# Small tables by TensorE transposes, and four modulation chunks as TensorE products, in a two-layer trunk kernel

## The chip, the cores and the metric

The kernel runs on one core of a Trainium2 chip. The metric is the time of one execution on the device in microseconds (us). The engines are named as the profile names them: PE (TensorE, with PEld its weight loads), DVE (VectorE), ACT (ScalarE), POOL (GpSimd) and SP (SyncE, which here only issues DMAs). ACTq and SPq are the instruction queues of ACT and SP with the DMAs that they issue. All data are float32.

## What is computed

The reference is a trunk of two layers on 256 tokens of 1024 channels. Each layer is modulated by six vectors of 1024 values, computed from one conditioning vector `c`:

```python
cond = jax.nn.silu(c)
for i in range(DEPTH):                                # 2
    mod = (cond @ mod_w[i] + mod_b[i]).reshape(B, 6, D_MODEL)   # mod_w[i] is 1024 x 6144
    h = modulate(rmsnorm(x, g[0]), mod[:, 0], mod[:, 1])        # shift, scale
    y = diff_attention(h, ...) if i == 0 else mlstm_layer(h, ...)
    x = x + mod[:, 2][:, None, :] * rmsnorm(y, g[1])
    h = modulate(rmsnorm(x, g[2]), mod[:, 3], mod[:, 4])
    y = swiglu(h, ...) if i == 0 else moe_swiglu(h, ...)        # 8 experts, top 2
    x = x + mod[:, 5][:, None, :] * rmsnorm(y, g[3])
```

The attention needs a scalar `lam_full`, made of exponentials of two sums over `attn_lambda`. The mLSTM layer multiplies its channels by three tables of 4x4 blocks (`mlstm_w_q`, `_k`, `_v`, 512 blocks each), and all three results by `mlstm_w_gate` (6144 x 8). The router of the experts is `moe_w_router` (1024 x 8).

## The kernel before

Five engine programs are written out by hand and meet at semaphores. All large weights come through one ring in SBUF of 7 slots of 2 MB (`ring`, `SLOTS`). `PLAN` lists the chunks in order, 512 columns of all 1024 rows each for the input matrices. It begins with four chunks of layer 0's `mod_w` (channels 0 to 2047, the first shift and scale), and then come the six chunks of the attention's input matrix, `attn_in` 0 to 5, with two more modulation chunks behind each of `attn_in` 0, 1 and 2 and one behind each of 3 and 4. Counted from 0, index 3 of `PLAN` is the fourth modulation chunk, 4 is `attn_in` 0, 7 is `attn_in` 1, 10 is `attn_in` 2, 13 is `attn_in` 3, 15 is `attn_in` 4 and 17 is `attn_in` 5. SP issues them strictly in that order (L418), and from the eighth on waits first until the chunk seven before has been read (L416).

The start runs as follows.

- SP (L403 to L413) loads the small vectors as rows of 128 (`rows`), eight DMAs, then `x`. PE turns `rows` (L794), DVE copies the result to `vecs` (L1242), and ACT makes `cond` of it with Silu (L550).
- ACT (L552 to L557) then issues seven DMAs: three tables of blocks (`qkv_blocks`, L553, runs of 4 floats), the gate weights (`w_gates`, L554, runs of 8 floats), the gate bias (L555), the router weights (`w_router`, L556, runs of 8 floats) and the router bias (L557). Only behind these stands in its program the exponential of the lambda step (L560), and behind that the squares of `x` and the scaling of `x` (L526, L530).
- DVE, after `vecs`, starts the lambda step (L1246, L1247), prepares some constants, waits for ACT's exponential and ends the lambda step (L1255 to L1257). Then come the variances (L1195) and the four modulation chunks (`mod_chunk`): eight instructions of 128x512 for each, a multiply (L1169) and seven multiply-adds (L1171) into `mod_acc`.
- PE sums each chunk's accumulator over the partitions with four 128x32 by 128x128 matmuls (`mod_sum`, L730), each in another group of 32 columns of the array, so that chunk j lands in row j of four row groups of PSUM bank 7. Then it turns the rows (`mod_turn`, L737), and the sixteen 128x128 tiles of the scaled `x` (`transposes`, L747). DVE adds the bias (L1185), makes `mul_c` (L1267) and writes the modulated, turned input `hT` (`modulated`, L1205).
- From there on PE multiplies the six `attn_in` chunks (L786 for 0 to 3, L815 for 4 and 5), 32 large matmuls each. A float32 matmul stands in the trace as two records, a transpose as one. Between the `attn_in` chunks PE sums the modulation chunks that DVE has accumulated meanwhile; the softmax stage follows.

The later stages (feed-forward, mLSTM, eight experts) are not touched, apart from what the semaphores count.

Of the kernel before, what the change touches and what calls it, by code (L numbers as in the profile page):

```python
# [19 lines left out]
ALU = mybir.AluOpType  # L20
# [6 lines left out]
P = 128  # L27
# [21 lines left out]
MOD_PARTS = {0: (0, 4, 12), 1: (0, 12)}  # L49

# [73 lines left out]
def trunk(nc, a, out):  # L124
    with ExitStack() as ctx:
# [26 lines left out]
        cond = sb("cond", [P, KT])  # L152
# [72 lines left out]

        hid = area(FT * S, after_acc).rearrange("p (k s) -> p k s", k=FT)
# [55 lines left out]
        cond_ready = sem("cond_ready")  # L282
        acc_ready = sem("acc_ready")
# [82 lines left out]
        for m, f, n, r in PLAN:  # L366
            j = f // WC
            if r == "dve":
                n_mod += 1
                read_by.append((acc_ready, n_mod))  # L370
# [30 lines left out]
        def sp_program(sp):  # L401

            sp.wait_ge(rows_clear, 1)  # L403
            cw = a["mlstm_conv_w"][0]
            sp.dma_start(rows[0:64, 0, :], cw.rearrange("j (t p) -> (j t) p", p=P)).then_inc(rows_loaded, 16)
# [3 lines left out]
            sp.dma_start(rows[0:8, 1, :], a["c"][0].rearrange("(t p) -> t p", p=P)).then_inc(rows_loaded, 16)  # L409
            sp.dma_start(rows[8:72, 1, :], a["norm_g"].rearrange("l i (t p) -> (l i t) p", p=P)).then_inc(rows_loaded, 16)  # L410
            sp.dma_start(rows[72:73, 1, :], a["attn_subln"]).then_inc(rows_loaded, 16)
            sp.dma_start(rows[0:96, 2, :], a["mod_b"].rearrange("l (t p) -> (l t) p", p=P)).then_inc(rows_loaded, 16)
# [21 lines left out]
        def pool_program(pool):  # L434
# [7 lines left out]
            pool.memset(rows, 0.0).then_inc(rows_clear, 1)  # L442
            pool.memset(exponent, -0.5)
# [52 lines left out]
            pool.wait_ge(small_loaded, 16 * 7)  # L496
# [15 lines left out]
        def act_program(act):  # L512
# [39 lines left out]
            for m, name in enumerate(("mlstm_w_q", "mlstm_w_k", "mlstm_w_v")):  # L552
                act.dma_start(qkv_blocks[:, m], a[name][0].rearrange("(t g) i o -> (g i) t o", g=P // 4)).then_inc(small_loaded, 16)  # L553
            act.dma_start(w_gates[:], a["mlstm_w_gate"][0].rearrange("(k p) n -> p k n", p=P)).then_inc(small_loaded, 16)  # L554
            act.dma_start(b_gates[:], a["mlstm_b_gate"].broadcast_to([P, 2 * MH])).then_inc(small_loaded, 16)  # L555
            act.dma_start(w_router[:], a["moe_w_router"][0].rearrange("(k p) n -> p k n", p=P)).then_inc(small_loaded, 16)  # L556
            act.dma_start(b_router[:], a["moe_b_router"].broadcast_to([P, E])).then_inc(small_loaded, 16)  # L557

            act.wait_ge(lam_ready, 1)
            act.activation(lam_e, lam_s, ACT.Exp).then_inc(lam_ready, 1)  # L560
            for t in range(TT):
                squares_x(0, t)
            for t in range(TT):
                normed_x(t, t + 1)

# [142 lines left out]
        def pe_program(pe):  # L708
# [15 lines left out]
            def mod_sum(layer, j, n):  # L724

                pe.wait_ge(acc_ready, n + 1)
# [5 lines left out]
                ins.then_inc(mod_summed, 1)  # L732

# [89 lines left out]
            pe.wait_ge(t_free, 2)  # L823

# [83 lines left out]
            def gate_products(t):  # L908
                pe.wait_ge(u_free, FILLS["qkv"] + 2 * (t + 1))
                if t == 0:  # L910
                    pe.wait_ge(small_loaded, 16 * 7)
                    pe.wait_ge(t_free, 5)
# [230 lines left out]
        def dve_program(dve):  # L1143
# [17 lines left out]
            def mod_chunk(layer, j, n):  # L1161
# [7 lines left out]
                link(dve.tensor_scalar(acc, w[:, 0], cond[:, 0:1], None, ALU.mult))  # L1169
                for k in range(1, KT):  # L1170
                    ins = dve.scalar_tensor_tensor(out=acc, in0=w[:, k], scalar=cond[:, k:k + 1], in1=acc,  # L1171
                                                   op0=ALU.mult, op1=ALU.add)
                    if k < KT - 1:
                        link(ins)
# [94 lines left out]
            modulated(0)  # L1269
            for j in range(6):  # L1270
# [408 lines left out]
```

## Time and profile before

| | before |
|---|---|
| median of 3 runs | 2170.09 us (2169.73 to 2179.38) |
| span of the profiled execution | 2170.9 us |
| PE busy | 1724.5 us, 79% |
| DVE busy | 474.3 us, 22% |
| ACT busy | 185.4 us, 9% |
| HBM read | 480.86 MB, 222 GB/s over the span |
| first matmul of `attn_in` starts | 89.44 us |
| first matmul of `attn_in` 3 starts | 132.42 us |

The result files give a time for each run, and the trace holds one more execution, whose span is given beside them. The page has each engine's busy share in 40 slices of 54.3 us, the chain of work that ended last, and the costliest groups of instructions. A group's "idle before" is the time its engine stood still ahead of it, with what ended the wait. The first slice is the one that the change touches, and it is read best instruction by instruction.

### The profile page before, as it was taken

The numbers are of one execution on the slowest core, as the hardware profiler recorded it, in microseconds if no ns is written. First come the engines' busy times: TensorE is split into PE (matmuls) and PEld (weight loads), VectorE is DVE, ScalarE is ACT, GpSimd is POOL, SyncE is SP. The second block draws the span as 40 slices with busy tenths as digits, with TensorE's granted clock in tenths as the row PEclk, the third lists the DMA queues.
The fourth block names the chain that finished last, engine by engine and source line by source line (L and its number), as shares of the span: only waits on it lengthen the run. The fifth ranks groups of instructions, "written<-read, shape, count | busy, mean of one in ns | idle before, by whom it ended". The sixth has DMA issues, their size and how long they took to land.

```text
span 2170.9 us, 18533 instructions
## 1 busy us (share of the span) xinstructions
PE 1724.5 (79%) x7558; PEld 1060.3 (49%) x7559; DVE 474.3 (22%) x1045; ACT 185.4 (9%) x404; POOL 33.2 (2%) x70
## 2 busy tenths in 40 slices
PE   0496799998978886687999968699996848768486
PEld 0374388844746633326996323299632313232232
DVE  0677235401563413101000000100001000100101
ACT  0104100001102101100000001000001001010010
POOL 0000000000020000000000000000000000000000
PEclk9997899999999887898999989999997979979798
DMA  9593239673401043397645429966651997969886
GB/s 300 179 379 140 78 144 342 218 283 117 155 1 39 0 160 111 140 402 278 220 166 198 152 82 336 396 238 227 237 195 55 396 368 268 402 243 399 324 309 252
DMA packets 219137, 484.72 MB, mean 223 GB/s; under 512 B 17545, under 2 KB 20002, under 8 KB 218914
## 3 DMA queue, kind: packets, MB, share of 16 engines
q1 hardware_dynamic: 205090, 481.46, 59.9%
q8 instruction: 118, 1.93, 0.4%
q10 hardware_dynamic: 13824, 0.47, 0.4%
q14 instruction: 105, 0.86, 0.1%
HBM read 480.86 MB, written 1.05 MB: 222 GB/s over the span
## 4 chain that ended last, share of the span: by engine, by line
PE 70%; issue 10%; DMA 8%; DVE 7%; ACTq 2%; ACT 1%; SPq 1%; POOL 0%; DVEq 0%; POOLq 0%
PE ps L786 15%; PE ps L1084 13%; PE ps L1054 13%; PE ps L1103 9%; DMA ring<-in_moe_w_down 7%; PE ps L773 6%; PE ps L1028 2%; PE ps L1131 2%; PE ps L815 1%; DMA ring<-in_moe_w_up 1%; DVE arena L1171 1%; ACTq L553 1%; PE ps L1063 1%; DVE hT L1205 1%; SPq L399 1%
## 5 line engine op out<-in xcount | busy, mean ns | idle before, releaser
L1054 PE MATMUL ps<-ring,arena 128*64 128x512 f32 x672 | 318.0, 631 | 47.9 <-issue 47.5
L1103 PE MATMUL ps<-ring,arena 128*64 128x512 f32 (+3 forms) x1120 | 322.6, 597 | 30.7 <-DMA ring<-in_moe_w_down 30.7
L786 PE MATMUL ps<-hT,ring 128*128 128x256 f32 x1472 | 327.3, 384 | 9.3 <-DVE hT L1205 7.6
L1055 PE MATMUL ps<-ring,arena 128*64 128x512 f32 x672 | 318.4, 631 | 0.0
L786 PEld LDWEIGHTS ps<-hT,ring 128*128 128x128 f32 x1472 | 281.4, 192 | 51.9 <-DVE hT L1205 8.8
L1084 PE MATMUL ps<-arena,ring 128*128 128x208 f32 (+1 forms) x1792 | 291.5, 326 | 0.0
L1084 PEld LDWEIGHTS ps<-arena,ring 128*128 128x128 f32 x1792 | 291.2, 190 | 0.0
L1103 PEld LDWEIGHTS ps<-ring,arena 128*64 128x64 f32 (+3 forms) x1120 | 110.2, 147 | 233.1 <-issue 179.5
L1054 PEld LDWEIGHTS ps<-ring,arena 128*64 128x64 f32 x672 | 94.1, 144 | 236.1 <-issue 234.3
L1028 PE MATMUL ps<-arena 128*128 128x128 f32 (+2 forms) x256 | 51.3, 384 | 151.1 <-issue 151.1
L773 PE MATMUL ps<-ring,arena 128*128 128x512 f32 x368 | 161.4, 601 | 1.5 <-DVE arena L1338 1.5
L1171 DVE SCALAR_TENSOR_TENSOR arena<-ring,cond,arena 128x512 f32<-128x512 f32 x168 | 126.3, 752 | 6.0
L1028 PEld LDWEIGHTS ps<-arena 128*128 128x128 f32 x256 | 49.5, 279 | 159.3 <-issue 159.2
L773 PEld LDWEIGHTS ps<-ring,arena 128*128 128x128 f32 x368 | 71.2, 194 | 92.2 <-issue 90.3
L1593 DVE TENSOR_TENSOR arena<-arena,ps 64x512 f32<-64x512 f32 x42 | 29.0, 690 | 360.7 <-ACT arena L645 360.7
L1055 PEld LDWEIGHTS ps<-ring,arena 128*64 128x64 f32 x672 | 94.1, 144 | 0.0
L1598 DVE TENSOR_TENSOR arena<-arena,ps 128x208 f32<-128x208 f32 (+1 forms) x56 | 19.9, 355 | 271.9 <-ACT arena L655 271.9
L730 PE MATMUL ps<-arena,ones_col 128*32 128x128 f32 x192 | 10.5, 306 | 72.3 <-DVE arena L1171 72.3
L1614 DVE TENSOR_TENSOR arena<-arena,ps 128x512 f32<-128x512 f32 x32 | 19.8, 682 | 215.0 <-PE ps L1131 215.0
L1587 DVE TENSOR_SCALAR arena<-ps,mul_c,modc 128x64 f32<-128x64 f32 (+2 forms) x64 | 21.2, 373 | 162.2 <-PE ps L1028 162.2
L1131 PE MATMUL ps<-arena 64*128 64x512 f32 (+3 forms) x80 | 44.3, 694 | 9.7 <-DVE arena L1606 5.3
L645 ACT ACTIVATE arena<-ps 64x512 f32<-64x512 f32 x42 | 24.8, 590 | 300.8 <-PE ps L1055 300.7
(262 smaller groups left out, 872.5 us busy)
## 6 DMA issues: line engine op xcount, KB each, us to landing
ring<-in_moe_w_gate SPq DMA_DIRECT2D x56, 2048.0 KB, 20.3
ring<-in_moe_w_up SPq DMA_DIRECT2D x56, 2048.0 KB, 18.8
ring<-in_moe_w_down SPq DMA_DIRECT2D x56, 2048.0 KB, 21.3
ring<-in_mod_w SPq DMA_DIRECT2D x24, 2048.0 KB, 11.9
ring<-in_mlstm_w_in SPq DMA_DIRECT2D x8, 2048.0 KB, 8.5
ring<-in_attn_w_in SPq DMA_DIRECT2D x6, 2048.0 KB, 10.5
ring<-in_ffn_w_gate SPq DMA_DIRECT2D x5, 2048.0 KB, 12.9
ring<-in_ffn_w_up SPq DMA_DIRECT2D x5, 2048.0 KB, 12.3
```

The lines of the kernel that those rows point to most:

```text
L399: sp.dma_start(slot_down(s), src).then_inc(landed[s], 16)
L645: act.activation(hx[0:width, j % 2, 0:WC], ps[0:width, 2 * (j % 2)], ACT.Silu).then_inc(silu_moe, STEP)
L773: ins = pe.matmul(ps[:, 4 + 2 * t + c], lhs[:, first + k, t * P:(t + 1) * P], w[:, k, c * 512:(c + 1) * 512], start=(first + k == 0), stop ...
L786: ins = pe.matmul(dst, w[:, k, c * P:(c + 1) * P], hT[:, k, :], start=(k == 0), stop=(k == KT - 1))
L1028: ins = pe.matmul(ps[:, i, j * S:j * S + wide], xn[:, t, k * P:(k + 1) * P], sel[:, t, 0:wide], start=(t == 0), stop=(t == TT - 1))
L1054: pe.matmul(ps[0:width, b], x_k, wg[:, k, :], start=(k == 0), stop=(k == KT - 1))
L1055: ins = pe.matmul(ps[low, b + 1], x_k, wu[:, k, :], start=(k == 0), stop=(k == KT - 1))
L1084: ins = pe.matmul(dst, w[:, k, c * P:(c + 1) * P], xg[:, k, 0:width], start=(k == 0), stop=(k == KT - 1))
L1103: ins = pe.matmul(ps[r, 4 + 2 * st + n], eh[:, ft, st * P:st * P + sw[st]], w[:, k, n * 512:(n + 1) * 512], start=(ft == 0), stop=(ft == E ...
L1131: ins = pe.matmul(ps[:, 4 + 2 * t + n], scat[0:sw[st], st, t * P:(t + 1) * P], ye[0:sw[st], st, n * 512:(n + 1) * 512], start=(st == 0), s ...
L1171: ins = dve.scalar_tensor_tensor(out=acc, in0=w[:, k], scalar=cond[:, k:k + 1], in1=acc, op0=ALU.mult, op1=ALU.add)
L1593: dve.tensor_tensor(hx[0:width, j % 2, 0:WC], hx[0:width, j % 2, 0:WC], ps[second_half(width), 2 * (j % 2) + 1], ALU.mult).then_inc(hx_rea ...
```

## The change

1. The seven small loads on ACT go to the head of its program, ahead of `cond`. Five of them change form: the blocks, the gate weights and the router weights are loaded as contiguous rows of 2 or 4 KB into scratch areas (16 rows for each of the three block tables, 48 for the gate weights, 8 for the router weights). PE turns them with 20 transposes (`turn_tables`: 4 + 8 + 8) into PSUM banks 4 and 5, reading every fourth or every eighth element of a row. ACT copies the result to the old tables in three instructions. A new semaphore holds back PE's softmax stage until these copies are done.
2. ACT's squares and scaling of `x` come ahead of the table copies and of the lambda exponential. DVE's end of the lambda step moves behind `modulated(0)`.
3. The first four modulation chunks are no longer accumulated by DVE. PE multiplies them directly (`mod_product`): for each of 8 row tiles and each of 4 column quarters a matmul of a 128x32 window of `cond` by 128x128 of the chunk. `cond` is for that widened to 63 columns per row tile with the values in column 31 and zeros around, set by two more POOL instructions. The transposes of `x` come between the first product and the second, the turned tables between the second and the third.
4. The eight loads of `rows` are issued in another order. The kernel is built with a smaller scratch area for DMAs issued by POOL, of which it has none.

```diff
+            for m, name in enumerate(("mlstm_w_q", "mlstm_w_k", "mlstm_w_v")):
+                act.dma_start(block_rows[IT * m:IT * (m + 1)],
+                              a[name][0].rearrange("(t g) i o -> t (g i o)", g=P // 4)).then_inc(tables_loaded, 16)
+            act.dma_start(table_rows[0:3 * IT], a["mlstm_w_gate"][0].rearrange("(k p) n -> k (p n)", p=P)).then_inc(tables_loaded, 16)
+            act.dma_start(router_rows[0:KT], a["moe_w_router"][0].rearrange("(k p) n -> k (p n)", p=P)).then_inc(tables_loaded, 16)
...
+            act.wait_ge(consts, 1)
             act.wait_ge(u_free, 1)
-            act.activation(cond[:], c_cols, ACT.Silu).then_inc(cond_ready, 1)
...
-            act.dma_start(w_gates[:], a["mlstm_w_gate"][0].rearrange("(k p) n -> p k n", p=P)).then_inc(small_loaded, 16)
...
+            act.activation(cond[:, :, 31], c_cols, ACT.Silu).then_inc(cond_ready, 1)
+            for t in range(TT):
+                squares_x(0, t)
+            for t in range(TT):
+                normed_x(t, t + 1)
+
+            act.wait_ge(tables_turned, 3)
...
             act.wait_ge(lam_ready, 1)
             act.activation(lam_e, lam_s, ACT.Exp).then_inc(lam_ready, 1)
-            for t in range(TT):
-                squares_x(0, t)
-            for t in range(TT):
-                normed_x(t, t + 1)
...
+            def mod_product(layer, j, n):
+
+                i = chunk(f"mod{layer}", j * WC)
+                w = slot_up(i % SLOTS)
+                for k in range(KT):
+                    for q in range(4):
+                        ins = pe.matmul(ps[32 * q:32 * (q + 1), 7, 0:P], cond[:, k, 31 - j:63 - j], w[:, k, q * P:(q + 1) * P],
+                                        start=(k == 0 and j in MOD_PARTS[layer]),
+                                        stop=(k == KT - 1 and j + 1 in MOD_PARTS[layer]))
+                ins.then_inc(mod_summed, 1)
+
+            def turn_tables():
+
+                pe.wait_ge(tables_loaded, 16 * 5)
+                for o in range(4):
+                    ins = pe.transpose(ps[:, 4, o * 3 * IT:(o + 1) * 3 * IT],
+                                       block_rows[0:3 * IT].rearrange("r (c o) -> r o c", o=4)[:, o], ident[0:3 * IT, 0:3 * IT])
+                ins.then_inc(tables_turned, 1)
...
-            mods = 0
-            for j in range(4):
-                mod_sum(0, j, mods)
-                mods += 1
+            pe.wait_ge(cond_ready, 1)
+            mod_product(0, 0, 0)
+            transposes_x(0)
+            mod_product(0, 1, 1)
+            turn_tables()
+            for j in range(2, EARLY):
+                mod_product(0, j, j)
+            mods = EARLY
             mod_turn(1)
-            transposes_x(0)
...
-            dve.wait_ge(lam_ready, 2)
-            link(dve.tensor_tensor(neg_lam, lam_e[:, 1:2], lam_e[:, 0:1], ALU.subtract))
-            link(dve.tensor_scalar(neg_lam, neg_lam, -LAMBDA_INIT, None, ALU.add))
             for t in range(TT):
                 variance(t)
             dve.wait_ge(cond_ready, 1)
-            mods = 0
-            for j in range(4):
-                mod_chunk(0, j, mods)
-                mods += 1
-
+            mods = EARLY
             modulation(1, 0, 4)
```

## Rows read from the trace of the kernel before

**Rows 1.** The page: its first line and the granted clock in 40 slices.

```profile
span 2170.9 us, 18533 instructions
PEclk9997899999999887898999989999997979979798
```

**Rows 2.** The chain that ended last, 0 to 150 us: start, us, what.

```profile
8.64 6.95 ACTq L553
15.62 11.47 ACTq L553
27.12 11.84 ACTq L554
38.99 14.27 ACTq L555
...
89.44 27.89 PE ps L786 x128
```

**Rows 3.** The timeline, 0 to 90 us: start, us, engine, line, what, idle before.

```profile
8.20 0.21 ACT L550 ACTIVATE cond<-vecs 128x8 f32<-128x8 f32 x1 [5.69 <-DVE vecs L1242]
...
54.40 1.28 ACT L560 ACT_TABLE_LOAD   x1 [45.99 <-issue]
...
56.00 0.16 DVE L1256 TENSOR_TENSOR small<-small 128x1 f32<-128x1 f32 x1 [46.06 <-ACT small L560]
...
57.88 2.29 ACT L530 ACTIVATE arena<-x,small 128x1024 f32<-128x1024 f32 x2
...
58.09 0.49 DVE L1169 TENSOR_SCALAR arena<-ring,cond 128x512 f32<-128x512 f32 x1
...
81.88 0.66 PE L730 MATMUL ps<-arena,ones_col 128*32 128x128 f32 x8 [5.26 <-DVE arena L1171]
82.60 0.29 DVE L1181 COPY arena<-ps 128x128 f32<-128x128 f32 x1 [0.78 <-PE ps L730]
...
83.22 3.62 PE L747 MATMUL ps<-ident,arena 128*128 128x128 f32 x16
...
83.67 0.17 DVE L1267 SCALAR_TENSOR_TENSOR mul_c<-modc,vecs 128x8 f32<-128x8 f32 x1
85.67 3.71 DVE L1205 TENSOR_SCALAR hT<-ps,mul_c,modc 128x256 f32<-128x256 f32 x8 [1.83 <-PE ps L747]
```

**Rows 4.** SP's chunk loads in index order, each with its issue and time to landing.

```profile
L418 SPq DMA_DIRECT2D ring<-in_mod_w x1: 460/460/460, 5.7 to 5.7; - x1
DMA to landing us min/median/max: 10.3/10.3/10.3
...
L418 SPq DMA_DIRECT2D ring<-in_mod_w x2: 5597/5754/5912, 6.9 to 12.5; - x2
DMA to landing us min/median/max: 21.2/21.4/21.6
...
L418 SPq DMA_DIRECT2D ring<-in_mod_w x2: 5894/5940/5987, 24.2 to 30.2; - x2
DMA to landing us min/median/max: 22.0/22.2/22.4
```

**Rows 5.** Stretches: us, busy of PE, PEld, DVE, ACT, POOL; clock, DMA share, GB/s.

```profile
10.00:50.00 40.00, 0.00 (x0) 0.00 (x0) 0.00 (x0) 0.00 (x0) 0.00 (x0) 1.00 1.10 355
120.00:145.00 25.00, 25.00 (x130) 21.63 (x129) 22.60 (x33) 0.00 (x0) 0.00 (x0) 1.00 1.05 389
150.00:155.00 5.00, 5.00 (x13) 2.26 (x12) 3.70 (x5) 0.00 (x0) 0.00 (x0) 1.00 1.02 408
163.00:217.00 54.00, 35.88 (x168) 23.02 (x167) 38.22 (x117) 24.09 (x102) 0.00 (x0) 0.78 0.38 139
```

**Rows 6.** The timeline, 103 to 176 us: the attention's input matrix and its end.

```profile
117.83 14.08 PE L786 MATMUL ps<-hT,ring 128*128 128x256 f32 x64
...
132.42 14.08 PE L786 MATMUL ps<-hT,ring 128*128 128x256 f32 x64
...
146.43 0.64 PE L730 MATMUL ps<-arena,ones_col 128*32 128x128 f32 x16
...
175.22 0.43 PE L730 MATMUL ps<-arena,ones_col 128*32 128x128 f32 x8
```

**Rows 7.** Groups of instructions, 0 to 180 us: the accumulations on DVE.

```profile
L1171 DVE SCALAR_TENSOR_TENSOR arena<-ring,cond,arena 128x512 f32<-128x512 f32 x84 | 63.2, 752 | 3.0
```

**Rows 8.** The router's matmuls, L1000: weight loads and their durations in ns.

```profile
L1000 PEld LDWEIGHTS ps<-w_router,hT x32: 288/333/338, 844.4 to 850.9; 128*128 128x128 f32 x32
```

More of the change, by code:

```diff
@@ L49 @@
 MOD_PARTS = {0: (0, 4, 12), 1: (0, 12)}
+EARLY = 4
 SLOTS = 7
@@ L151, in trunk @@
         gate_c = sb("gate_c", [P, 4, KT])
-        cond = sb("cond", [P, KT])
+        cond = sb("cond", [P, KT, 63])
         qkv_blocks = sb("qkv_blocks", [P, 3, IT, 4])
@@ L224, in trunk @@
         lam_in = area(4 * DA).rearrange("p (i n) -> p i n", i=4)
+        table_rows = o_nat[:, 0, :]
+        block_rows = o_nat[:, 1, 0:512]
+        router_rows = oT.rearrange("p k s -> p (k s)")[:, 0:D]
         hid = area(FT * S, after_acc).rearrange("p (k s) -> p k s", k=FT)
@@ L282, in trunk @@
         cond_ready = sem("cond_ready")
+        tables_loaded = sem("tables_loaded")
+        tables_turned = sem("tables_turned")
+        tables_ready = sem("tables_ready")
         acc_ready = sem("acc_ready")
@@ L404, in sp_program @@
             cw = a["mlstm_conv_w"][0]
+            sp.dma_start(rows[0:8, 1, :], a["c"][0].rearrange("(t p) -> t p", p=P)).then_inc(rows_loaded, 16)
+            sp.dma_start(rows[8:72, 1, :], a["norm_g"].rearrange("l i (t p) -> (l i t) p", p=P)).then_inc(rows_loaded, 16)
+            sp.dma_start(rows[72:73, 1, :], a["attn_subln"]).then_inc(rows_loaded, 16)
+            sp.dma_start(rows[0:96, 2, :], a["mod_b"].rearrange("l (t p) -> (l t) p", p=P)).then_inc(rows_loaded, 16)
             sp.dma_start(rows[0:64, 0, :], cw.rearrange("j (t p) -> (j t) p", p=P)).then_inc(rows_loaded, 16)
@@ L442, in pool_program @@
             pool.memset(rows, 0.0).then_inc(rows_clear, 1)
+            pool.memset(cond[:, :, 0:31], 0.0)
+            pool.memset(cond[:, :, 32:63], 0.0)
             pool.memset(exponent, -0.5)
@@ L564, in act_program @@
                 normed_x(t, t + 1)
+            act.wait_ge(tables_turned, 3)
+            act.activation(qkv_blocks.rearrange("p m t o -> p (m t) o"),
+                           ps[:, 4, 0:4 * 3 * IT].rearrange("p (o k) -> p k o", o=4), ACT.Copy)
+            act.activation(w_gates[:], ps[:, 5, 0:8 * 3 * IT].rearrange("p (n k) -> p k n", n=2 * MH), ACT.Copy)
+            act.activation(w_router[:], ps[:, 5, 384:384 + E * KT].rearrange("p (n k) -> p k n", n=E), ACT.Copy).then_inc(tables_ready, 1)
+            act.wait_ge(lam_ready, 1)
+            act.activation(lam_e, lam_s, ACT.Exp).then_inc(lam_ready, 1)
             def exps(h):
@@ L732, in mod_sum @@
                 ins.then_inc(mod_summed, 1)
+            def mod_product(layer, j, n):
[13 more added lines that the diff above has]
+                ins.then_inc(tables_turned, 1)
+                for n in range(2 * MH):
+                    ins = pe.transpose(ps[:, 5, n * 3 * IT:(n + 1) * 3 * IT],
+                                       table_rows[0:3 * IT].rearrange("r (c n) -> r n c", n=2 * MH)[:, n], ident[0:3 * IT, 0:3 * IT])
+                ins.then_inc(tables_turned, 1)
+                for e in range(E):
+                    ins = pe.transpose(ps[:, 5, 384 + e * KT:384 + (e + 1) * KT],
+                                       router_rows[0:KT].rearrange("r (c e) -> r e c", e=E)[:, e], ident[0:KT, 0:KT])
+                ins.then_inc(tables_turned, 1)
             def mod_turn(n):
@@ L823, in pe_program @@
             pe.wait_ge(t_free, 2)
+            pe.wait_ge(tables_ready, 1)
             def scores(h):
@@ L1168, in mod_chunk @@
                 acc = mod_acc[:, n % 2]
-                link(dve.tensor_scalar(acc, w[:, 0], cond[:, 0:1], None, ALU.mult))
+                link(dve.tensor_scalar(acc, w[:, 0], cond[:, 0, 31:32], None, ALU.mult))
                 for k in range(1, KT):
-                    ins = dve.scalar_tensor_tensor(out=acc, in0=w[:, k], scalar=cond[:, k:k + 1], in1=acc,
+                    ins = dve.scalar_tensor_tensor(out=acc, in0=w[:, k], scalar=cond[:, k, 31:32], in1=acc,
                                                    op0=ALU.mult, op1=ALU.add)
@@ L1269, in dve_program @@
             modulated(0)
+            dve.wait_ge(lam_ready, 2)
+            link(dve.tensor_tensor(neg_lam, lam_e[:, 1:2], lam_e[:, 0:1], ALU.subtract))
+            link(dve.tensor_scalar(neg_lam, neg_lam, -LAMBDA_INIT, None, ALU.add))
             for j in range(6):
```

23 lines of the change are left out of this document (7 added, 16 removed).

## The prediction

> **What bounds the kernel now.** I read the page first. Its span is 2170.9 us, and the median of the runs shown is 2170.09 us, so the profiled execution stands for them within 0.04%; I make the sum against its span and take 0.8 us off at the end. The change touches only what lies ahead of the softmax stage, so the second view is the chain that ended last, read for the first 150 us. There the reader sees 44.6 us, from 8.64 to 53.28 us, in four issues of DMAs on ACT's queue (6.95 + 11.47 + 11.84 + 14.27 and small gaps) [rows 2]. No engine computes in that time. The third view is the timeline of the same stretch. ACT had made `cond` at 8.4 us, but the next instruction in its program that computes stands behind the seven issues and begins at 54.40. DVE waits 46.06 us for the lambda exponential, and so its four modulation chunks, whose first begins at 58.09, come late too [rows 3]. Each takes some 5.9 us: 0.49 for the first instruction and seven of 752 ns with their gaps [rows 3, 7]. The first `attn_in` matmul starts at 89.44 us [rows 2]. The idle wait and the four accumulations thus stand one behind the other, and both are on the path.
>
> The fourth view is the loads. Chunk 0 is issued at 5.7 and lands 10.3 us later, at 16.0. Index 2 lands at 28.1 (6.9 + 21.2), index 3 at 34.1 (12.5 + 21.6), index 5 at 46.2 and index 6 at 52.6 (30.2 + 22.4) [rows 4]. Once both waits of above are gone, this is what is late next.
>
> **The small loads (part 1).** They are the 16-byte and 32-byte pieces that block ACT's queue. As whole rows there are 16 + 16 + 16 + 48 + 8 of them, each 2 or 4 KB, and the two bias loads keep their form. I take the issue cost per DMA as small as that of SP's first chunk, 0.46 us [rows 4], which makes 3.2 us for seven from about 1.2 us on, over before DVE's `vecs` at 8.2 us, on which `cond` waits [rows 3]. So what they cost beside the rows' loads is nothing; if that cover is gone, see the third rival. They take 44.6 us off ACT.
>
> **The lambda step and the squares (part 2).** The squares and the scaling of `x` then run right behind `cond`, some 4 us for the four instructions and POOL's powers between them (the scaling alone took 2.29 us [rows 3]). `xn` is ready near 16 us, as chunk 0 lands. On DVE the end of the lambda step is two short instructions (one took 0.16 us [rows 3]); in its new place DVE waits for the first `attn_in` result anyway, so I cost it at nothing, and at 0.4 us without that cover. The exponential comes behind the table copies on ACT, near 30 us, and is asked for near 40.
>
> **The products (part 3).** They remove 4 x 5.9 = 23.6 us of DVE work and four `mod_sum`. They add 32 matmuls of 128x32 by 128x128 a chunk. The nearest row is `mod_sum` itself, four such matmuls side by side: 0.66 us after an idle wait, 0.43 us in the midst of work, and 0.64 us for eight of them in the midst of work [rows 3, 6]. The second four thus add 0.21 us. A product of eight fours costs between 0.43 + 7 x 0.21 = 1.9 us and 8 x 0.66 = 5.3 us. I take 2.5 us, near the lower end, since PE will be working with short pauses from 16 us on. The granted clock in this stage is 1.00 in every stretch that I read [rows 5], so the 0.66 against 0.43 does not show in that column. The Trainium skill, "TensorE: Matmul & The Clock Gate", section on the HAM clock gate, says that after idling the array runs at 1.2 GHz until it has been busy; the durations agree with that, the column does not show it. By that rule all products of a PE that keeps pausing would be near the upper end, which is the second rival.
>
> **The turned tables.** The 20 transposes have no row of their own, for they read every fourth or eighth element. The sixteen of `x` took 3.62 us, 0.226 each [rows 3]; the dearest weight load of 128 columns in a short matmul took 0.338 [rows 8]. So 4.5 to 6.8 us, and 4.5 is taken. They stand between the second and the third product. PE's sum to the end of the third product is 16.0 + 3 x 2.5 + 3.6 + 4.5 = 31.6 us. The fourth chunk lands no earlier than that (below), so PE's own work is hidden behind the loads, by little. ACT's three copies delay nobody: PE asks for them only in the softmax stage. `cond`'s two more memsets on POOL, and the new order of the rows' loads, are hidden by the rows' landing and cost nothing.
>
> **The loads, new pace.** While the small pieces were in the queues the core moved 355 GB/s; without them, with the same kind of chunks, 389 GB/s, and 408 for others [rows 5]. A chunk of 2.097 MB thus takes 5.39 us, between 5.14 and the 6.1 of the landings in the present start, (52.6 - 16.0) / 6 [rows 4]. I take 5.39, from the row with the same matrices. Index i then lands at 16.0 + 5.39 i: index 3 at 32.2, index 4 at 37.6, 7 at 53.7, 10 at 69.9, 13 at 86.1, 15 at 96.9.
>
> **The new start.** The fourth product ends at 32.2 + 2.5 = 34.7. From the end of the last `mod_sum` (82.54) to the end of `mul_c` (83.84) are 1.3 us; then `hT` takes 3.71, and no transposes stand between them any more [rows 3]. With the gaps that is 5.1 us, so the first `attn_in` matmul starts at 39.8 instead of 89.44: 49.6 us earlier.
>
> **What is given back.** In the present kernel the four chunks stood in the ring long before, and PE went through `attn_in` at its own pace: the first two took 27.89 us, `attn_in` 3 started at 132.42, and the stage ended at 175.7 [rows 2, 6]. Now PE asks for three chunks' worth of loads each 14.6 us, and they take 16.2. By PE's pace `attn_in` 1, 2 and 3 start at 53.8, 68.2 and 82.8; by the loads no earlier than 53.7, 69.9 and 86.1. DVE frees index 6's slot at about 54.5 + 2 x 5.9 = 66.3, ahead of the time at which SP's queue would carry index 13, so this wait costs nothing. `attn_in` 3 starts at 86.1, 3.3 us of the gain are gone, and from there the loads run ahead again (`attn_in` 4 is asked for at 100.7 and lands at 96.9). The gain is 132.42 - 86.1 = 46.3 us. It then stays: in the softmax stage the loads need 0.38 of their time [rows 5], so the ring fills up in either kernel, and what follows is the same.
>
> **Sum.** 2170.9 - 46.3 = 2124.6 us of span, 2124 us as a median. Bounds: at 5.14 us a chunk PE's pace decides and 49.6 are gained, at best 2120; if also the product costs 1.9, 2119.
>
> **Rivals.**
> - *The loads stay at the pace of the present start*, 6.1 us a chunk, because it was never the small pieces that slowed them. Index 13 lands at 16.0 + 79.3 = 95.3, the gain is 37.1, the time 2133 us. For it: the 355 GB/s stood for 40 us [rows 5]. Against it: 389 and 408 in the same kernel. The Trainium skill, "DMA: Bandwidth & Descriptors", section "Specifications", gives some 358 GB/s as the limit of HBM per core; this trace disagrees with 389 and 408 GB/s. Chance 0.15.
> - *PE is slow in the start.* Products of 5.3 us and transposes of the tables of 6.8: 16.0 + 4 x 5.3 + 3.6 + 6.8 + 5.1 = 52.7. From there PE's pace decides, `attn_in` 3 starts at 95.7, gain 36.7, 2133 us. For it: the row after an idle wait. Against it: the pauses are short. Chance 0.1.
> - *The loads on ACT block it as before.* `cond` now stands behind them; if they took 44.6 us from 1.2 us on, `cond` would come at about 46, and 46 + 10 + 3.6 + 4.5 + 5.1 = 69.2 as the start, a gain of 20, 2150 us. Against it: 104 whole rows in place of thousands of pieces. Chance 0.04.
> - *Slower than before: the fours don't run side by side and each matmul pays a full weight load.* Place: the 128 matmuls of the products, ahead of all. Price: two records of up to 0.338 us each [rows 8], 0.676 a matmul, 86.5 us in all, a start at 16.0 + 86.5 + 3.6 + 4.5 + 5.1 = 115.7 and 2196 us. It decides from 0.47 us a matmul on ((89.44 - 29.2) / 128). Against it: four in 0.43 to 0.66 us [rows 3, 6]. Chance 0.02.
> - The granted clock of the later stages differs from slice to slice of the page, 7 to 9 tenths [rows 1], 0.78 in the softmax stage [rows 5]; it moves the runs shown by up to 9 us. This widens the range and is no case of its own.
>
> **Chances.** Forecast 0.69, the rivals 0.15, 0.1, 0.04, 0.02. A measurement of this kernel can tell about 0.5% (10.9 us) from no change. The forecast and the first three rivals are faster by more than that, less a little for cases between the third and the fourth: faster 0.95, within 0.5% 0.03, slower 0.02. The range takes in both bounds of the load's pace, the second rival and some of the runs' spread: 2116 to 2137 us.
>
> **What would show it.** The first `attn_in` matmul near 40 us and `attn_in` 3 near 86; products of 2 to 3 us each; the wait ahead of the fourth product ended by a DMA; PE waiting one to two us for a chunk ahead of `attn_in` 2 and of 3; 385 GB/s or more from 10 to 100 us; an unchanged time from the softmax stage to the end. It is wrong if ACT still spends over 10 us on issues, if PE waits for `tables_loaded`, if products take over 5 us, or if the later stages differ by more than 5 us.

## The result

| | before | changed |
|---|---|---|
| median | 2171.86 us (2169.73 to 2179.38, 4 runs) | 2124.24 us (2123.46 to 2129.76, 4 runs) |
| ratio to before | | 0.9777, 95% interval 0.9754 to 0.9800 |
| span of the profiled execution | 2170.9 us | 2122.3 us |
| `attn_in` starts | 89.44 us | 42.24 us |
| `attn_in` 3 starts | 132.42 us | 87.81 us |
| `attn_in` 4 starts | 147.00 us | 102.40 us |

The kernel is 47.6 us faster by the medians and 48.6 us by the spans. The four long issues of DMAs on ACT's queue [rows 2] are gone, and all seven now take 3.4 us, from 1.21 to 4.57 us. The timeline of the changed kernel, 0 to 60 us (columns as in [rows 3]), shows what stands in their place:

```profile
3.11 0.58 ACTq L563 DMA_DIRECT2D arena<-in_moe_w_router  x1
...
10.71 0.21 ACT L569 ACTIVATE cond<-vecs 128x8 f32<-128x8 f32 x1
...
15.87 3.64 PE L758 MATMUL ps<-ring,cond 128*32 128x128 f32 x64 [7.13 <-DMA ring<-in_mod_w]
19.44 2.32 PE L792 MATMUL ps<-ident,arena 128*128 128x128 f32 x16
21.69 1.95 PE L758 MATMUL ps<-ring,cond 128*32 128x128 f32 x64
23.57 0.68 PE L767 MATMUL ps<-ident,arena 48*128 48x48 f32 x4
24.09 1.04 PE L771 MATMUL ps<-ident,arena 48*128 48x48 f32 x8
25.06 1.04 PE L775 MATMUL ps<-ident,arena 8*128 8x8 f32 x8
...
28.15 3.64 PE L758 MATMUL ps<-ring,cond 128*32 128x128 f32 x64 [2.05 <-DMA ring<-in_mod_w]
33.57 3.64 PE L758 MATMUL ps<-ring,cond 128*32 128x128 f32 x64 [1.78 <-DMA ring<-in_mod_w]
37.35 0.29 DVE L1230 COPY arena<-ps 128x128 f32<-128x128 f32 x1 [24.17 <-PE ps L758]
...
38.48 3.71 DVE L1254 TENSOR_SCALAR hT<-ps,mul_c,modc 128x256 f32<-128x256 f32 x8
```

L758 are the products, L792 the transposes of `x`, L767 to L775 the turned tables. The reader is to see that the third and the fourth product waited for a DMA; the loads are now what the start waits for. The same kind of product takes 1.95 us once and 3.64 us three times. The stretches (columns as in [rows 5]) show the granted clock beside that, and that the loads run at full pace throughout:

```profile
15.84:19.50 3.66, 3.63 (x65) 3.28 (x65) 0.00 (x0) 0.00 (x0) 0.00 (x0) 1.00 1.06 388
...
21.69:23.60 1.91, 1.91 (x66) 1.71 (x65) 0.00 (x0) 0.00 (x0) 0.00 (x0) 1.00 1.05 387
...
28.15:31.80 3.65, 3.64 (x64) 2.98 (x64) 0.00 (x0) 0.33 (x2) 0.00 (x0) 0.50 1.05 387
33.57:37.20 3.63, 3.63 (x64) 2.96 (x64) 0.00 (x0) 0.00 (x0) 0.00 (x0) 0.50 1.04 385
42.24:47.00 4.76, 4.76 (x11) 3.86 (x12) 0.17 (x2) 0.00 (x0) 0.00 (x0) 0.50 1.05 387
```

At 0.50 the array runs at 1.2 GHz, at 1.00 at 2.4. The first product, behind 7.13 us of waiting, took 3.64 us too, but the column reads 1.00 beside it: there the column and the duration don't agree. The first `attn_in` matmuls, behind a wait of 4.22 us, ran at 0.50 as well: the first two chunks took 30.48 us in place of 27.89 [rows 2].

### The profile page after: what moved, and what is told of

It is laid out like the page before. It is cut to its first block, busy times and chain, and to the rows that moved or that the text cites. A ratio compares the mean times of both kernels' runs of the same rounds, so it can differ in the third digit from the quotient of the medians.

```text
span 2122.3 us, 18995 instructions
## 1 busy us (share of the span) xinstructions
PE 1728.3 (81%) x7802; PEld 1072.5 (51%) x7803; DVE 451.6 (21%) x1013; ACT 186.3 (9%) x407; POOL 33.3 (2%) x72
## 3 DMA queue, kind: packets, MB, share of 16 engines
q8 instruction: 120, 1.97, 0.5%
## 4 chain that ended last, share of the span: by engine, by line
PE 72%; issue 11%; DMA 8%; DVE 6%; ACT 1%; SPq 1%; POOL 1%; DVEq 0%; ACTq 0%; POOLq 0%
PE ps L831 15%; PE ps L1103 14%; PE ps L1133 14%; PE ps L1152 9%; DMA ring<-in_moe_w_down 7%; PE ps L818 7%; PE ps L1077 2%; PE ps L1180 2%; PE ps L863 1%; DMA ring<-in_mod_w 1%; PE ps L1112 1%; DVE hT L1254 1%; SPq L407 1%; PE ps L1104 1%; PE ps L804 1%
## 5 line engine op out<-in xcount | busy, mean ns | idle before, releaser
L1220 DVE SCALAR_TENSOR_TENSOR arena<-ring,cond,arena 128x512 f32<-128x512 f32 x140 | 105.3, 752 | 5.0
L487 POOL TENSOR_TENSOR small<-small 128x1 f32<-128x1 f32 (+2 forms) x21 | 15.5, 737 | 1973.0 <-DVE small L1244 1698.1
L1180 PE MATMUL ps<-arena 64*128 64x512 f32 (+3 forms) x80 | 37.7, 607 | 9.7 <-DVE arena L1651 5.3
```

What stands on the lines that cost most here:

```text
L1180: ins = pe.matmul(ps[:, 4 + 2 * t + n], scat[0:sw[st], st, t * P:(t + 1) * P], ye[0:sw[st], st, n * 512:(n + 1) * 512], start=(st == 0), s ...
```

## The experiments

"The changed kernel" is the one of the diff. Once `attn_in` 4 has started, TensorE waits for no further chunk of this matrix in any of the kernels, so its time sums up the start. Each set of runs had its own runs of the kernel before, whose medians are 2171.86 to 2173.78 us. The column "loads of code" is the packet count of the page's instruction queue (q8).

| kernel | median us | ratio, 95% interval | `attn_in` starts | `attn_in` 3 | `attn_in` 4 | loads of code |
|---|---|---|---|---|---|---|
| before | 2171.86 to 2173.78 | 1 | 89.44 | 132.42 | 147.00 | 118 |
| changed | 2124.24 | 0.9777 (0.9754 to 0.9800) | 42.24 | 87.81 | 102.40 | 120 |
| keep_busy | 2148.11 | 0.9884 (0.9869 to 0.9899) | 40.53 | 87.65 | 102.24 | 127 |
| shift_mods | 2128.17 | 0.9788 (0.9772 to 0.9804) | 40.41 | 85.60 | 100.18 | 120 |
| busy_and_shift | 2144.22 | 0.9864 (0.9849 to 0.9879) | 40.24 | 83.00 | 98.36 | 127 |
| tables_only | 2131.01 | 0.9807 (0.9790 to 0.9824) | 45.85 | 91.80 | 106.38 | 119 |
| pad_only | 2129.22 | 0.9794 (0.9780 to 0.9807) | 41.16 | 87.47 | 102.05 | 120 |
| busy_padded | 2146.98 | 0.9873 (0.9858 to 0.9888) | 40.48 | 87.62 | 102.20 | 127 |
| both_padded | 2144.11 | 0.9865 (0.9850 to 0.9881) | 40.44 | 83.20 | 98.48 | 127 |
| moved_code | 2147.88 | 0.9880 (0.9865 to 0.9895) | 40.46 | 87.61 | 102.20 | 127 |
| old_form_last | 2135.47 | 0.9823 (0.9810 to 0.9837) | 42.66 | 95.21 | 109.80 | 120 |
| reorder_only | 2135.00 | 0.9830 (0.9813 to 0.9848) | 45.48 | 95.18 | 111.45 | 118 |
| both_few | 2123.22 | 0.9765 (0.9752 to 0.9779) | 40.42 | 83.19 | 98.43 | 120 |

### How much of the gain belongs to the products

tables_only: all of the change but the products.

```diff
+            for j in range(4):
+                mod_chunk(0, j, mods)        # DVE, as before
...
-            mod_product(0, 0, 0)
             transposes_x(0)
-            mod_product(0, 1, 1)
             turn_tables()
-            for j in range(2, EARLY):
-                mod_product(0, j, j)
+            for j in range(4):
+                mod_sum(0, j, mods)
```

> The changed kernel without its products: loads as whole rows, turned tables, lambda step and squares in their new places, but VectorE accumulates the first four modulation chunks again (23.6 us of work). If that work stood on the path in full, the time is some 20 us above that of the changed kernel. If it hides behind the landing of the chunks, only the last accumulation shows: chunk 3 lands at 33.5, VectorE ends it at 39.4, attn_in starts at about 45.2 instead of 42.2, attn_in 3 at about 90 instead of 87.8, and the kernel is 2 to 3 us slower than the changed one (2127 us). I expect the second: then most of the gain is that of the tables and the order on ScalarE's queue.

Measured: 2131.01 us, `attn_in` from 45.85 us. The second theory held in its number: the work of 23.6 us does not stand on the path in full. It runs beside the landing of the chunks, at nearly the same pace. DVE waits for the first chunk (until 16.32 us) and for no other; it works on the four without a break, 5.9 us each, while the fourth lands at 32.5. Its last multiply-adds run from 34.57 to 40.05 us (timeline of this kernel), so it ends 7.5 us behind the fourth landing, one chunk's work and some 1.5 us by which it had fallen behind.

```profile
34.57 5.48 DVE L1218 SCALAR_TENSOR_TENSOR arena<-ring,cond,arena 128x512 f32<-128x512 f32 x7
```

The products are worth 102.40 against 106.38, 4 us, in the start. At the end tables_only is 6.8 us above the changed kernel and 1.8 above its second set of runs (pad_only, below), where 2 to 3 were expected; the runs do not tell the end-to-end value more closely than that.

reorder_only: neither turned tables nor products, only another order on ACT and DVE. In old_form_last the products stay, and only the tables go back to the old form.

```diff
             act.activation(cond[:, :, 31], c_cols, ACT.Silu).then_inc(cond_ready, 1)
+            # squares and scaling of x, then the lambda exponential
+            for m, name in enumerate(("mlstm_w_q", "mlstm_w_k", "mlstm_w_v")):
+                act.dma_start(qkv_blocks[:, m], a[name][0].rearrange("(t g) i o -> (g i) t o", g=P // 4)).then_inc(small_loaded, 16)
+            # ... and the four others, as in the kernel before
```

> No turned tables and no products: the kernel before with the old-form loads issued last on ScalarE, the squares and lambda step ahead of them, and VectorE's end of the lambda step behind the modulated input. Forecast by the loads: chunks land every 6 us, the fourth at 34, VectorE accumulates it until 40, attn_in starts at 46; index 13 lands at about 94, attn_in 3 starts there, and some 38 of the 48 us are gained, 2133 us. If the accumulations (23.6 us) or the small loads still stood on the path in full, it would be 2145 us or more.

> The changed kernel, but the small tables are loaded straight to their places in the old form (16-byte and 32-byte pieces), issued last on ScalarE's queue, behind cond, the squares, the scaling and the lambda exponential; no turned tables (ten tiny matmuls take the place of their code). If what counts is only that nothing waits behind these loads, the time is that of the changed kernel, 2124 to 2129 us. If the pieces slow the chunk loads as in the kernel before (355 instead of 387 GB/s, 6.1 instead of 5.5 us a chunk), the fourth chunk lands at 34 to 35 us, index 13 at 93 to 95 instead of 87.6, and the time is 5 to 7 us above the changed kernel. I expect the second.

Measured: 2135.00 and 2135.47 us. The forecast by the loads held in reorder_only (`attn_in` 3 at 95.18), and the second theory in old_form_last. The order alone brings 38.8 us (2173.78 - 2135.00) of the 47.6 that the changed kernel gains, or of the 44.3 that its program gains in pad_only. old_form_last is 6.3 us above pad_only, as expected, and 11.2 above the changed kernel's own runs. What the old form costs is seen in the loads. The stretches are those of 50 to 90 us, of old_form_last and of the changed kernel:

```profile
50.00:90.00 40.00, 36.11 (x173) 30.72 (x172) 25.99 (x37) 0.00 (x0) 0.00 (x0) 0.96 1.10 353
```

```profile
50.00:90.00 40.00, 40.00 (x212) 34.45 (x211) 28.49 (x41) 0.00 (x0) 0.00 (x0) 1.00 1.05 387
```

353 against 387 GB/s, and TensorE of old_form_last waits for chunks ahead of `attn_in` 1, 2 and 3:

```profile
59.08 14.08 PE L823 MATMUL ps<-hT,ring 128*128 128x256 f32 x64 [0.44 <-DMA ring<-in_attn_w_in]
77.19 15.77 PE L823 MATMUL ps<-hT,ring 128*128 128x256 f32 x64 [3.45 <-DMA ring<-in_attn_w_in]
95.21 14.08 PE L823 MATMUL ps<-hT,ring 128*128 128x256 f32 x64 [1.69 <-DMA ring<-in_attn_w_in]
```

The small pieces thus slow the large loads even where nobody waits for them. How much of the DMA engines' time they take is seen in the queue that carries ACT's loads (packets, MB, share of the 16 engines' time), 0 to 60 us, of the kernel before and of the changed one; the bytes are the same:

```profile
q10 hardware_dynamic: 13824, 0.47, 15.8%
```

```profile
q10 hardware_dynamic: 608, 0.47, 3.9%
```

The Trainium skill, "DMA: Bandwidth & Descriptors", section "Specifications", puts the smallest transfer for line rate at 512 bytes; the pieces have 16 and 32, and the trace agrees. Its 358 GB/s for HBM per core, which the prediction weighed as a rival, is exceeded for 80 us on end in the changed kernel (387 and 389).

### Loads or TensorE's pace

keep_busy fills TensorE's waits in the start; shift_mods lets the `attn_in` chunks come earlier in the loads; busy_and_shift does both.

```diff
             turn_tables()
-            for j in range(2, EARLY):
-                mod_product(0, j, j)
+            keep_busy(12, 6)                 # transposes of ident into an unused bank
+            mod_product(0, 2, 2)
+            keep_busy(22, 6)
+            mod_product(0, 3, 3)
             mods = EARLY
             mod_turn(1)
+            pe.wait_ge(tables_ready, 1)
+            keep_busy(28, 4)
```

```diff
-MODS = {0: [[4, 5], [6, 7], [8, 9], [10], [11], []], ...
+MODS = {0: [[4], [5, 6], [7, 8], [9, 10], [11], []], ...
```

> The changed kernel, with transposes of the identity that nobody reads put where TensorE waits in the start: 12 ahead of the third product, 22 ahead of the fourth, 28 behind the turn of the modulation rows. In the changed kernel the third and fourth product took 3.64 us each at a granted clock of 0.50, and the first attn_in matmuls ran at 0.50 too. Clock theory: the idle stretches are the cause, all four products but the first take 1.95 us, and attn_in starts at 40.5 instead of 42.2 us and runs at its full pace at once. What that is worth is where two theories part. If TensorE's own pace sets the time of attn_in 3, it starts at about 83.5 instead of 87.8 us and the kernel gains some 4.3 us. If the loads set it (index 13 landed at 87.6), attn_in 3 still starts at about 87.7 and the kernel gains nothing. I expect the second.

> The changed kernel with one line changed: the eight modulation chunks between the attn_in chunks stand one place later, 1, 2, 2, 2, 1 instead of 2, 2, 2, 1, 1, so that attn_in 1, 2 and 3 have index 6, 9 and 12 of the loads instead of 7, 10 and 13. If the loads alone set the time of attn_in 3, it starts some 5.5 us earlier (82 us). If TensorE's pace sets it as well, it starts at 87.8 as before and nothing is gained. I expect the second: in the changed kernel TensorE ended attn_in 2 just as index 13 landed.

> Both edits at once. If loads and TensorE tie in the changed kernel, as the expectations of the two single edits say, then both together give what neither gives alone: attn_in starts at 40.5, attn_in 3 at about 83.5, index 12 lands at about 82, and the kernel is 4.3 us faster than the changed one. If either of them alone was the bound, the pair gives no more than the better of the two.

Measured in the start: as expected for keep_busy and for both edits together; shift_mods, where nothing was expected, gained 2.2 us. Kept busy, TensorE begins `attn_in` at 40.53, runs the first chunk in 14.08 us, and waits for the loads (timeline of keep_busy):

```profile
71.41 14.08 PE L831 MATMUL ps<-hT,ring 128*128 128x256 f32 x64 [1.57 <-DMA ring<-in_attn_w_in]
...
87.65 2.64 PE L831 MATMUL ps<-hT,ring 128*128 128x256 f32 x11 [1.59 <-DMA ring<-in_attn_w_in]
```

So in the changed kernel the loads and a half-clocked TensorE come out even at `attn_in` 3, 87.8 us. keep_busy alone gains nothing there, and both edits together gain 4.8 us (`attn_in` 3 at 83.00). shift_mods won 2.2 us on its own, because the fourth product happened to run at full clock there (1.96 us) and the start came at 40.41; from there to `attn_in` 3 are 45.2 us, TensorE's pace with the slow beginning (45.6 in the changed kernel). An early start without the shift wins nothing: moved_code, below, starts `attn_in` at 40.46 and waits 1.36 us for the chunk of `attn_in` 3, which starts at 87.61.

Measured at the end: not as expected at all. Both kernels with the 62 added transposes lose 20 to 24 us against the changed kernel (15 to 19 against pad_only, its second set of runs), though their starts are as early or earlier. That needed theories of its own.

### What the added transposes cost

> The kernel with kept-busy TensorE started earlier, as expected, and was still some 24 us slower than the changed kernel; the loss lies from the mLSTM stage on (5 us) and in the experts (3.5 us for each of five narrow ones, with pauses that the profile puts down to issue). This run is the changed kernel with 124 empty instructions at the head of TensorE's program, where TensorE idles until 7.8 us. They do no work, and only move all later instructions by as many places as the 62 added transposes did. Placement theory: the loss comes from where the later code lies, so the start is that of the changed kernel (attn_in at 42.2) and the time is 2144 us or more, 20 us above the changed kernel. Activity theory: the loss comes from TensorE's added work and its clock; then this run equals the changed kernel, 2124 us. I expect the first.

> The kernel with kept-busy TensorE plus 132 empty instructions at the head of TensorE's program, so that the later code is moved by 256 places in all. The instruction loads in the page move some 16 KB each, which is 256 instructions of 64 bytes; if the placement matters by its offset in such a piece, this kernel has the placement of the changed one. Placement theory: the experts take the changed kernel's time again, attn_in starts at 40.5, the loads still set attn_in 3, and the time is within 2 us of the changed kernel (2122 to 2126 us). Activity theory: it stays at 2147 us.

> Kept-busy TensorE, the shifted modulation chunks and the 132 empty instructions. With the changed kernel's placement restored the 4 us that the start had gained (attn_in 4 started at 98.4 instead of 102.4 us) should reach the end: 2120 us, 4 us below the changed kernel. If placement is not the cause of the loss: 2143 us.

```diff
+            for _ in range(124):             # 132 in the other two
+                pe.nop()
             pe.wait_ge(consts, 1)
             pe.wait_ge(rows_loaded, 16 * 8)
```

Measured: 2129.22, 2146.98 and 2144.11 us, the times of the kernels without the empty instructions. TensorE's compiled program has the same size with and without them (1,735,488 bytes in pad_only and in the changed kernel), so they left no code. The three expectations failed with their premise, and the runs decide between neither theory. Two things came out of them. They are repeats: pad_only is the changed kernel's program once more, 5 us slower at the median. And they sent me to the instruction loads: 120 and 127, in the page's list of DMA queues (packets, MB, share) of the changed kernel and of keep_busy:

```profile
q8 instruction: 120, 1.97, 0.5%
```

```profile
q8 instruction: 127, 2.08, 0.5%
```

moved_code adds code, but next to no work:

```diff
             mods = EARLY
             mod_turn(1)
+            pe.wait_ge(tables_ready, 1)
+            for _ in range(31):
+                pe.matmul(ps[0:32, 4, 0:1], ident[:, 0:32], ident[:, 0:1], start=True, stop=True)
```

> The empty instructions of the two padded kernels left no code: their pages count as many instruction loads as the kernels without them (120 and 127), so they decided nothing and were repeats. The kept-busy kernel has 127 such loads of 16 KB against 120 in the changed kernel, seven more, as many as there are experts after the first. This run is the changed kernel with 31 tiny matmuls (32 columns by 1) where TensorE waits 4 us for the modulated input. Each is four instructions, so the later code moves by 124, just as in the kept-busy kernel, for about a microsecond or two of work. Placement theory: 127 instruction loads, narrow experts of 136 instead of 132.5 us, 2146 us. Activity theory: 120 loads and the changed kernel's time, 2124 to 2129 us. I expect the first.

Measured: 2147.88 us and 127 loads. The start is that of the changed kernel (`attn_in` 4 at 102.20), the loss comes later, and all seven loads more fall behind 800 us, where the experts are (103 against 96). Each expert runs one of several bodies of code, by the number of its tokens: six of the eight the narrow one (64 columns), two a wide one (208 and 176). The loss shows where a narrow expert is entered; the expert's first matmuls, moved_code:

```profile
1750.81 1.65 PE L1080 MATMUL ps<-arena 128*128 128x128 f32 x6 [26.31 <-issue]
1755.50 5.08 PE L1080 MATMUL ps<-arena 128*128 128x128 f32 x26 [3.04 <-issue]
```

and the changed kernel:

```profile
1738.15 6.58 PE L1077 MATMUL ps<-arena 128*128 128x128 f32 x32 [26.03 <-issue]
```

One more stop, here of 3.04 us, stands behind the sixth record. It occurs in each of the six narrow experts of moved_code, of 1.4 to 3.0 us, and in neither of the two wide ones. The trace also holds the packets of the instruction queue. From 1752.4 to 1755.5 us, the stop of above, there is one of q8:

```profile
q8 instruction: 1, 0.02, 2.2%
```

It runs from 1752.95 to 1754.05 us. In all six narrow experts the stop ends 1.3 to 1.6 us after such a load, and it is the longer the later the load came: 1.4 to 1.9 us where the load began 0.5 to 1.1 us after the first matmul, 2.2 us where it began after 1.2, and 3.0 us where it began after 2.1 to 2.3. In pad_only, the same program as the changed kernel, the load behind the entry stands at the same distance (0.5 to 2.5 us) and nothing stops. What TensorE waits for there is thus the load of code. From the pages of pad_only and moved_code, the line of these matmuls (count | busy, mean ns | idle before):

```profile
L1079 PE MATMUL ps<-arena 128*128 128x128 f32 (+2 forms) x256 | 53.1, 394 | 152.9 <-issue 152.9
```

```profile
L1080 PE MATMUL ps<-arena 128*128 128x128 f32 (+2 forms) x256 | 56.2, 403 | 166.8 <-issue 166.8
```

That is 13.9 us more waiting, in 14 waits in place of 8, and 3.1 us more of work: 17.0 of the 18.3 us by which the two spans differ (2146.4 and 2128.1). The other 1.3 us arise ahead of the router. Three narrow experts near the end take 134.5, 136.7 and 135.5 us from the first matmul of one to that of the next in moved_code, and 132.2, 132.9 and 132.7 in the changed kernel. The activity theory falls. That the place of the code decides, and not its mere amount, rests on the changed kernel itself: its TensorE program is 31,360 bytes longer than that of before and needs two loads more on q8, while 7,936 bytes on top of that cost seven. (The other queue of instruction loads, q14, counts 105 before, 112 in the changed kernel and 112 in moved_code. So a higher count there went with no loss: the same three narrow experts take 132.0, 132.2 and 132.6 us before.) The Trainium skill, "Runtime: NRT & Kernel Launch", section "Terms", says that the instruction memory is refilled in blocks of 16 KiB; 1.97 MB in 120 packets agrees. Which offset in a block does the harm is open: sizes of TensorE's program of 192, 1,088, 2,816, 15,104 and 15,168 bytes beyond a multiple of 16,384 were harmless, 6,720 was not.

both_few does the work of keep_busy with nine matmuls of 512 columns, 36 instructions in place of 124, and keeps the shifted chunks:

```diff
+                    pe.matmul(ps[:, b], ident[:], x[:, 0, 0:512], start=True, stop=True)
...
+            keep_busy(2, 6)   # ahead of the third product; 3 ahead of the fourth, 4 behind the turn
```

> Kept-busy TensorE and shifted modulation chunks again, but the added work is nine matmuls of 512 columns (36 instructions) in place of 62 transposes (124 instructions): two ahead of the third product, three ahead of the fourth, four behind the turn of the modulation rows. Placement theory: the code moves so little that the instruction loads stay at 120, the experts take the changed kernel's time, and the 4 us gained in the start (attn_in 4 at 98.4 instead of 102.4 us) reach the end: 2118 to 2121 us. Activity theory: 2144 us, as with the 62 transposes.

Measured: 120 loads, `attn_in` 4 at 98.43, all products but the first at 1.95 or 1.96 us, and 2123.22 us: 21 us below the same idea with 62 transposes, as the placement theory says. The 4 us of the start did not reach the end for certain, and the median lies above the 2118 to 2121 us expected. Against pad_only, the same program as the changed kernel, both_few is faster (0.9765 against 0.9794, the intervals part by a hair), against the changed kernel's own runs it is not. It is no version that I would call better.

### Do the four matmuls run side by side

```diff
-                        ins = pe.matmul(ps[32 * q:32 * (q + 1), 7, 0:P], cond...
+                        g = 0 if k else q
+                        ins = pe.matmul(ps[32 * g:32 * (g + 1), 7, 0:P], cond...
```

> The changed kernel, but of each product only the first four matmuls go to the four column groups, and the other 28 all to the first. The first four modulation chunks are thus wrong sums in this kernel; the work is the same in number and shape. Theory of the prediction: the products are short because four matmuls run side by side. Then the product grows from 1.95 us (full clock) or 3.64 us (half clock) to between 6 and 13 us, TensorE and no longer the loads sets the start, and attn_in starts at 55 us or later; the kernel loses over 8 us. Rival: each matmul costs its issue and small weight load only, and the column group does not matter. Then the products keep 1.95 and 3.64 us and the time stays.

Measured: the second product takes 6.52 us at a granted clock of 1.00, against 1.95, and `attn_in` starts at 53.23 (55 or later was expected), `attn_in` 4 at 113.18.

```profile
26.48 6.52 PE L759 MATMUL ps<-ring,cond 128*32 128x128 f32 x64
```

The side-by-side theory holds. Its wrong sums send tokens to other experts, so its 2144.90 us can't be read as a whole; up to the router the loss is 10 us (808.04 against 798.07 us in pad_only).

## Why the prediction was right

The time was forecast at 2124 us and is 2124.24. Its steps, one by one:

- **The bound before** and the idle wait on ACT: right (on the accumulations see below), and the gain at the first matmul is 47.2 us (49.6 forecast).
- **Issues on ACT**: 3.4 us for seven (3.2). `cond` came at 10.9 instead of 8.4 us: the rows' last load was waited for until 7.86 us, 1.2 us longer than before, and the Silu table load of 1.28 us stands in ACT's way now. I had not seen either; chunk 0 landed at 15.8 us and hid both.
- **Products**: 2.5 us were put down; 1.95 at full and 3.64 at half clock were measured, between the bounds. The fourth one, on the path, took 3.64.
- **Turned tables**: 2.5 us for 20 (23.57 to 26.10), less than the lower bound of 4.5. That bound was taken from transposes at 0.226 us each, which in the changed kernel take 0.145 and in keep_busy 0.123. The durations say that the row of before was of a slow array, although its granted clock reads 1.00.
- **Loads**: index 3 landed at 33.5 (32.2 forecast), index 13 at 87.6 (86.1), 5.52 us a chunk (5.39). From index 3 to 13 it was 5.41; the first three behind chunk 0 took 17.7 us, 1.5 more than forecast. The slot of index 13 came free at 71.4 us, not 66.3 as forecast, because DVE first copied a result of `attn_in` 0, for which it waited until 58.95, and began on the two chunks at 59.55 and not 54.5; the loads went on at 387 GB/s and it cost nothing.
- **The chain to `attn_in`**: 5.0 us (5.1).
- **What is given back**: the place was right and the mechanism half right. I forecast TensorE waiting for loads; in the changed kernel's profile it does not. It started `attn_in` 2.4 us later than forecast, and its half-clocked beginning took 2.6 us more, which was not in the sum. By these 5.0 us its own pace moved from 82.8 to 87.8, just behind the landing of index 13 at 87.6. keep_busy, where TensorE is on time, shows the forecast waits, 1.57 and 1.59 us, and the same program as the changed kernel's in pad_only, whose first two chunks took 29.63 us, shows one of 1.52 ahead of `attn_in` 3. `attn_in` 3 started at 87.81 (86.1).
- **It stays to the end**: 44.6 us at `attn_in` 4, against 46.3 forecast, and 48.6 at the end. The missing 4.0 us come from two later stages, and not from the change. Feed-forward input and mLSTM before its output matrix take 166.29 and 241.15 us in the changed kernel's profile, 168.93 and 243.79 in pad_only's, which is the same program, and 169.67 and 243.94 before; the granted clock goes the same way, 0.99 and 0.92, 0.98 and 0.91, 0.97 and 0.91. These two stages are 6.2 us shorter than before, and the rest takes 2.2 of it back. That the forecast hits the median within 1 us is thus partly luck, of a few us.

Two things the prediction had in substance wrong, though the sum came out. It put the 23.6 us of DVE's accumulations "on the path", as the idle wait is, and had the products remove them. Its own later step, the landing of the chunks, contradicts that, and it did not ask what the time would be without the products: 4 us more in the start. And it took the later stages as unchanged ("what follows is the same"), without a rival for the place of the code. moved_code shows what stood at stake there: 19 to 24 us, nearly half of the gain, for 7,936 bytes of code more.

The rivals: the pace of 6.1 us a chunk did not come about, but its number did where its cause was put back, in old_form_last (`attn_in` 3 at 95.21; 95.3 forecast). The slow-TensorE one came true in part, with products at 3.64 and not 5.3 us. The blocked queue did not occur. The serial products did not; forced into one column group they cost some 0.20 us a matmul, and the point at which they would have been slower than before, 0.47 us, is far off.

## What to carry to other kernels

Before a slow engine's work is rewritten for a faster one, ask when its input lands: here all but 4 of 23.6 us of accumulation ran beside the loads, and a mere reordering, small loads last on their queue, brought some four fifths of the gain. Small pieces of 16 or 32 bytes cost twice, once on the queue of the engine that issues them and once in the bandwidth of the large loads beside them. In a kernel whose loop bodies are some hundreds of kilobytes of instructions (here 96 loads of 16 KB behind 800 us, for eight experts), look at the count of instruction loads in the page after each edit, even one far away. If it jumps, look for stops behind the entry of a body: the count alone proves no loss.

## What the hardware did that I had not expected

- Adding 124 TensorE instructions in the start brought seven more loads of code (127 in place of 120) and a stop of 1.4 to 3.0 us behind the sixth matmul record of every narrow expert, which ends 1.3 to 1.6 us after a load of code. From the first matmul of a narrow expert to that of the next expert it takes 1.4 to 4.0 us longer than in pad_only.
- The granted clock read 0.50 in the third and the fourth product of the changed kernel, behind waits of 2.05 and 1.78 us between short bursts of work. It is not the same each time: behind like waits the fourth product took 1.95 us in moved_code, 1.96 in shift_mods and 2.65 in pad_only, which is the changed kernel's program. Behind 4.2 us of waiting ahead of `attn_in` the first two chunks took 29.63 to 30.86 us in six kernels (30.63 in moved_code, whose tiny matmuls left a wait of 2.16), and 27.89 in the three with filler and the shift, so the slow beginning costs 1.7 to 3.0 us. The Trainium skill, "TensorE: Matmul & The Clock Gate", section "Part 1: The HAM clock gate", says that idling lowers the clock to 1.2 GHz; the column shows it here as 0.50. In the kernel before, the column read 1.00 while transposes took 0.226 us instead of 0.145, and in the changed one while the first product took 3.64 us, so a 1.00 behind a long idle stretch is not to be trusted.
- The same program gave medians of 2124.24 and 2129.22 us in two sets of runs. Differences below 5 us need the two kernels side by side in one set.
